# Up projection of a gated MLP: one 512-column matmul over both halves of the activation, and a convolution that reads SBUF

## The reference

```python
def dwconv2d_grid(x, w):
    B, T, C = x.shape
    rows = T // GRID_W                        # GRID_W = 64
    y = lax.conv_general_dilated(x.reshape(B, rows, GRID_W, C), w[:, :, None, :],
                                 window_strides=(1, 1), padding=((1, 1), (1, 1)),
                                 dimension_numbers=('NHWC', 'HWIO', 'NHWC'),
                                 feature_group_count=C)
    return y.reshape(B, T, C)

def conv_glu_ffn(h, w_up, conv_w, w_down, grid):
    up = h @ w_up                             # (256, 2048) @ (2048, 11264)
    up = dwconv2d_grid(up, conv_w)
    a, b = jnp.split(up, 2, axis=-1)
    return (jax.nn.silu(a) * b) @ w_down      # (256, 5632) @ (5632, 2048)
...
h2 = rmsnorm(x, g_pre2) * (1.0 + sc2) + sh2
x = x + gt2 * rmsnorm(conv_glu_ffn(h2, w_up, conv_ffn, w_down, grid=True), g_post2)
```

## Time and profile before

| | |
|---|---|
| median of the runs | 2902.12 us |
| the profiled execution | 2901.94 us, span 2899.9 us |
| TensorE busy | 2783.1 us, 96% |
| VectorE busy | 1893.0 us, 65% |
| ScalarE busy | 996.5 us, 34% |
| GpSimd busy | 567.7 us, 20% |
| TensorE clock granted, mean | 0.982 of full |
| up stage | from 2111.8 us to 2626.9 us |

### The profile page before, as it was taken

One profiled execution on the slowest core, in us unless ns is written; L12 is line 12 of the kernel. 1 busy time (PEld: TensorE's weight loads), 2 busy tenths in 40 slices (PEclk: granted clock), 3 DMA queues, 4 the chain that ended last, 5 costly groups with the idle time before them and its releaser, 6 DMA issues.

```text
span 2899.9 us, 66324 instructions
## 1 busy us (share of the span) xinstructions
PE 2783.1 (96%) x25890; PEld 2094.7 (72%) x25890; DVE 1893.0 (65%) x3509; ACT 996.5 (34%) x1684; POOL 567.7 (20%) x708
## 2 busy tenths in 40 slices
PE   5899999999999999999988999999899999999997
PEld 1346666656666665666655888887789999998886
DVE  1136776666777666777675656564588999896444
ACT  1133333233333223333221433333344444443332
POOL 0012322223321222331220200000023333330000
PEclk8899999999999999999999999999999999999999
DMA  8721233321223322223234545554535555554554
GB/s 329 325 81 57 89 103 110 104 97 57 88 96 110 110 96 65 83 88 110 81 105 157 191 163 193 181 188 168 187 123 182 186 178 186 177 184 160 185 183 138
DMA packets 75801, 412.84 MB, mean 142 GB/s; under 512 B 9296, under 2 KB 11984, under 8 KB 42608
## 3 DMA queue, kind: packets, MB, share of 16 engines
q1 hardware_dynamic: 74864, 408.10, 40.5%
q0 software_dynamic: 768, 2.10, 0.2%
HBM read 405.38 MB, written 4.19 MB: 141 GB/s over the span
## 4 chain that ended last, share of the span: by engine, by line
PE 90%; DVE 4%; DMA 2%; ACT 2%; issue 1%; SPq 0%; DVEq 0%; ACTq 0%; PEldq 0%
PE PB L714 21%; PE Q L977 12%; PE Q L972 6%; PE PB L972 4%; PE PB L967 4%; PE CH L972 3%; PE PB L968 3%; PE CH L967 3%; PE CH L968 3%; PE Q L850 3%; PE Q L836 3%; DMA ring<-w_mod_dram 2%; PE Q L857 2%; PE CH L891 2%; PE CH L873 2%; PE CH L901 1%
## 5 line engine op out<-in xcount | busy, mean ns | idle before, releaser
L714 PE MATMUL PB<-hT,ring 128*128 128x512 f32 (+1 forms) x1536 | 670.7, 551 | 1.0
L1703 DVE TENSOR_TENSOR w_lo_r<-ring,w_hi_r 128x1536 fp32r<-128x1536 f32 (+3 forms) x178 | 389.9, 2190 | 204.4 <-ACT w_hi_r L1290 204.4
L1290 ACT ACTIVATE w_hi_r<-ring 128x2048 fp32r<-128x2048 f32 (+2 forms) x178 | 325.8, 1830 | 314.2 <-PE PB L972 104.0
L714 PEld LDWEIGHTS PB<-hT,ring 128*128 128x128 f32 x1536 | 256.1, 189 | 114.3 <-issue 69.8
L968 PE MATMUL PB<-hT_r,w_hi_r 128*128 128x256 f32 x832 | 204.7, 286 | 0.0
L1989 POOL TENSOR_TENSOR w_lo_r<-ring,w_hi_r 128x512 fp32r<-128x512 f32 x88 | 118.1, 1342 | 356.9 <-ACT w_hi_r L1290 356.9
L1878 DVE TENSOR_TENSOR w_lo_r<-ring,w_hi_r 128x1408 fp32r<-128x1408 f32 x62 | 100.7, 1626 | 131.9 <-ACT w_hi_r L1409 131.9
L1558 DVE SCALAR_TENSOR_TENSOR arena<-ring,csilp,arena 128x512 f32<-128x512 f32 x240 | 180.5, 752 | 6.1 <-DMA ring<-w_mod_dram 1.5
L967 PE MATMUL PB<-hT_r,w_hi_r 128*128 128x256 f32 x704 | 175.9, 289 | 2.8 <-DVE hT_r L1805 2.8
L977 PE MATMUL Q<-ff_r,w_hi_r 128*128 128x512 f32 x704 | 174.4, 395 | 3.5 <-ACT w_hi_r L1409 3.5
L967 PE MATMUL CH<-hT_r,w_hi_r 128*128 128x256 f32 x704 | 170.9, 283 | 0.0
(11 more groups left out here) (268 smaller groups left out, 5335.8 us busy)
## 6 DMA issues: line engine op xcount, KB each, us to landing
ring<-w_up_dram SPq DMA_DIRECT2D x88, 1024.0 KB, 4.8
ring<-w_mod_dram SPq DMA_DIRECT2D x128, 512.0 KB, 3.6
ring<-w_rkv_dram SPq DMA_DIRECT2D x48, 1024.0 KB, 6.0
ring<-w_down_dram SPq DMA_DIRECT2D x64, 704.0 KB, 4.0
ring<-w_mod_dram SPq DMA_DIRECT2D x32, 1024.0 KB, 9.3
ring<-w_ga_dram SPq DMA_DIRECT2D x16, 1024.0 KB, 4.8
ring<-w_gb_dram SPq DMA_DIRECT2D x16, 1024.0 KB, 4.9
ring<-w_pa_dram SPq DMA_DIRECT2D x16, 1024.0 KB, 4.9
```

The costliest lines, as they stand in the source:

```text
L714: last = mm(PB[slot % 2][:, 0:cols], tile(n, kt), hT[:, kt, 0:cols], start=(kt == 0), stop=(kt == KT - 1))
L1290: f(w_hi_r[:, r % 2, 0:n], ring[:, r, 0:n], ACT.Copy).then_inc(hi_rdy, 1)
L1703: tt(w_lo_r[:, r, 0:n], ring[:, r, 0:n], as_f32(w_hi_r[:, r % 2, 0:n]), ALU.subtract).then_inc(lo_rdy, 1)
```

## The change

Each tile of the up stage takes its high part by 16 matmuls of 512 columns over both parts of the activation (columns 0 to 255 of the bank get high·low, columns 256 to 511 high·high), and the low part is added in columns 256 to 511. ScalarE copies columns 0 to 255 into a new SBUF buffer `us[r]` (memory of `woven_sb`), and VectorE adds columns 256 to 511 to it (`add_halves`). The centre tap (ScalarE) and the eight other taps (VectorE) then read `us[r]` in SBUF. TensorE gets the bank back after that addition (`up_sum`). Before a pair's centre taps ScalarE waits for both additions.

```diff
+        us = [woven_sb[:, r].rearrange("p c t -> p (c t)")[:, 0:T] for r in range(4)]
...
-                    pe.wait_ge(up_cv, i * 2 + 1 + r // 2)
+                    pe.wait_ge(up_sum, i * 4 + r + 1)
                     for kt in range(KT):
                         if first and r == 0:
                             pe.wait_ge(h_rdy, KT + kt + 1)
-                        with_high(four[r][:, 0:T], r, kt, h2_hi_r[:, kt], h2_lo_r[:, kt], kt == 0)
+                        mm(four[r][:, :], w_hi_r[:, r % 2, kt * P:(kt + 1) * P], hT_r[:, kt], start=(kt == 0), stop=False)
...
-                        last = with_low(four[r][:, 0:T], r, kt, h2_hi_r[:, kt], kt == KT - 1)
+                        last = with_low(four[r][:, T:TT], r, kt, h2_hi_r[:, kt], kt == KT - 1)
...
                     if r % 2 == 0:
+                        act.wait_ge(up_cv, i * 2 + r // 2 + 1)
+                    f(us[r], four[r][:, 0:T], ACT.Copy).then_inc(up_half, 1)
+                    if r % 2:
                         act.wait_ge(ff_rdy, i * 2 + r // 2 + 1)
-                    f(cv[r], four[r][:, 0:T], ACT.Identity, scale=convw_a[:, r, 4:5]).then_inc(up_mid, 1)
+                        for q in (r - 1, r):
+                            act.wait_ge(up_sum, i * 4 + q + 5)
+                            f(cv[q], us[q], ACT.Identity, scale=convw_a[:, q, 4:5]).then_inc(up_mid, 1)
...
-                        last = stt(grid(cv[r])[:, orow, ocol], grid(four[r][:, 0:T])[:, irow, icol],
+                        last = stt(grid(cv[r])[:, orow, ocol], grid(us[r])[:, irow, icol],
                                    convw_v[:, r, w:w + 1], grid(cv[r])[:, orow, ocol], ALU.mult, ALU.add)
...
+            def add_halves(i, r):
+
+                dve.wait_ge(up_half, i * 4 + r + 1)
+                tt(us[r], us[r], four[r][:, T:TT], ALU.add).then_inc(up_sum, 1)
...
                 if carry is not None:
                     dve.wait_ge(dve_step, V.base)
                     taps(i - 1, 1, 1, carry)
+                add_halves(i, 0)
+                add_halves(i, 1)
                 lows("up", i, 0, FT // 2, "down")
...
                 taps(i, 0, 1, prev)
+                add_halves(i, 2)
+                add_halves(i, 3)
                 lows("up", i, 2, FT // 2, "down")
```

More of the change, by code:

```diff
@@ L354, in layer_kernel @@
         xr_ld = sem("x_reloaded")
+        up_half = sem("up_low_activation_half_copied")
+        up_sum = sem("up_halves_added")
         up_mid = sem("up_centre_tap_done")
@@ L1068, in _ @@
             pe.sem_inc(up_cv, 2)
+            pe.sem_inc(up_sum, 4)
             pe.sem_inc(ff_rdy, 2)
@@ L1813, in taps @@
             def taps(i, j, half, prev):
-                if half == 0:
-                    dve.wait_ge(up_mid, i * 4 + 2 * j + 2)
                 for n in range(4 * half, 4 * half + 4):
@@ L1823, in taps @@
                         ocol, icol = slice(max(0, -b), GRID - max(0, b)), slice(max(0, b), GRID - max(0, -b))
-                        if n:
+                        if n == 0:
+                            dve.wait_ge(up_mid, i * 4 + r + 1)
+                        else:
                             V.need(prev[q])
                         w = 3 * (a + 1) + b + 1
-                        last = stt(grid(cv[r])[:, orow, ocol], grid(four[r][:, 0:T])[:, irow, icol],
+                        last = stt(grid(cv[r])[:, orow, ocol], grid(us[r])[:, irow, icol],
                                    convw_v[:, r, w:w + 1], grid(cv[r])[:, orow, ocol], ALU.mult, ALU.add)
```

## The result

The changed kernel takes 2952.8 us (median of 4 runs, 2951.37 to 2955.72), beside 2902.2 us of the kernel before in the same comparison: ratio 1.0171, 95% interval 1.0157 to 1.0185, or 50.6 us more. Forecast were 2963 us and a range of 2915 to 2992. The profiled execution took 2955.72 us, with a span of 2952.8.

The account below looks back on a forecast made before the run. TensorE bounds the up stage before; then VectorE, 19.9 us of work plus 6.0 for GpSimd, 25.9 us a group against 23.04. Over 22 groups 63 us, less 3, plus 1: +61, so 2963 us, range 2915 to 2992.

Parts of the forecast that it names:

- TensorE's part: Up stage: wider matmuls give back 0.19 us a tile, 17 us over 22 groups, if TensorE stays the bound.
- VectorE's own work: Up stage: 18.5 us of present work plus 1.4 of new additions make 19.9 us a group.
- The price of the additions: Up stage: four new additions a group at 0.34 us each, 1.36 us a group, all on VectorE's line.
- Taps out of SBUF exclude GpSimd: Up stage: VectorE taps with both tensors in SBUF and GpSimd instructions reading SBUF shut each other out for the whole instruction.
- For nearly every GpSimd instruction: Up stage: 18.4 of VectorE's 19.9 us need both tensors from SBUF, so nearly every GpSimd instruction costs its full price.
- GpSimd's term: Up stage: four weight parts at 1.08 us and two activation splits at 0.25 + 0.58 cost VectorE 6.0 us a group.
- The upper bound of the term: GpSimd's cost to VectorE in the up stage is at most 6.6 us a group, cast 0.40, weight parts 1.14 each.
- The ends: Up stage: 3 us taken off for the first and last groups, 1 us added at the end for the last taps.
- Signs that were forecast: Up stage: VectorE never idle, TensorE about 86% busy, GpSimd's weight parts 1.4 to 1.7 us, some taps 0.8 to 1.5.
- Half the price: Rival: weight parts cost 0.54 us each, GpSimd 3.8 us a group in the up stage; +15 us, 2917 us; chance 0.12.
- TensorE stays the bound: Rival: GpSimd costs at most 2.14 us a group, VectorE needs 22.0 against 22.28; 17 us faster, 2885 us; chance 0.08.
- slower than the sum: Rival: SBUF taps cost 0.03 us more each, GpSimd 6.6 us a group; +94 us, 2996 us; chance 0.06.

Follow-up runs that it names:

- e3: Kernel before with the 512-column matmuls alone, high weight by low activation left out, no additions: 2886.35 us, ratio 0.9944 to the kernel before.
- e1: Changed kernel with the sum of the halves written back into PSUM, where all taps read it: 2887.62 us, ratio 0.9954 to the kernel before.
- e5: Kernel before plus one VectorE addition for each tile, into a buffer nobody reads: 2906.29 us, ratio 1.0004.
- e8: Changed kernel without GpSimd's weight parts, four matmuls reading the first four blocks instead: 2889.58 us, ratio 0.9949 to the kernel before.
- e2: Kernel before, with ScalarE also copying each tile into SBUF, where the eight taps read it; no additions: 2926.66 us, ratio 1.0086.
- e6: Changed kernel with VectorE making all 2048 columns of each low part and GpSimd none: 2910.78 us, ratio 1.0024 to the kernel before.
- e7: Changed kernel with 1024 instead of 512 columns of each low part on GpSimd: 3002.09 us, ratio 1.0338 to the kernel before.

## Why the prediction was right, and where its sizes were off

- *TensorE's part* (0.19 us a tile, 17 us): right. e3 measured 16 us, and the groups of e1 are 22.27 us apart where 22.28 were forecast.
- *VectorE's own work* (19.9 us a group): right. 25.3 less the 5.4 of stretched taps leave 19.9, and e1, where nothing is stretched, has VectorE busy for 19.9 us a group.
- *The price of the additions*: they cost nothing alone (e5), since VectorE's line stays under TensorE's 23.04 us.
- *Taps out of SBUF exclude GpSimd*: right; e1 takes it away by the place, e8 by the other side, and e2 makes it alone. *For nearly every GpSimd instruction*: right. In the changed kernel each of them stretches a tap.
- *GpSimd's term* (6.0 us a group) was too large: it is 5.4. A weight part costs a tap 1.45 - 0.41 = 1.04 us (forecast 1.08), the subtraction 0.89 - 0.41 = 0.48 (0.58), the cast 0.61 - 0.47 = 0.14 (0.25, chosen without a row). 4 x 1.04 + 2 x 0.48 + 2 x 0.14 = 5.4. Over 22 groups the difference is 13 us. The upper bound of the term was added up a little too high: 4 x 1.14 and 2 x 0.98 are 6.5 us and not 6.6.
- *The ends* were too small in both directions, and partly made up for each other. The first and last groups gave back 4.3 us (45.2 instead of 49.5) where 3 were taken off, and behind the up stage came 5.8 us where 1 was put on. The longer wait at the start of the down stage and the lower clock behind it are in no term of the sum. That the forecast is only 10 us from the result, with 13 us too much in the groups, owes something to that.
- *Signs that were forecast*: VectorE without idle time, TensorE waiting for low parts, the other taps at 0.41 us, the clock at 1.00 within the up stage, all seen. A tap beside a cast takes 0.61 us, under the forecast 0.8. TensorE busy for 86% was not a good sign. The window has 92%, in part because matmul records overlap (0.39 us each at a pace of 0.23), so that the last one before a wait reaches into it. By tiles it is 4 x 5.57 of 25.3 us, 88%. GpSimd's weight parts at 1.4 to 1.7 us hold for three of four, and the fourth mostly takes 4.99 us.
- *Half the price* failed because the weight parts meet taps and not splits; *TensorE stays the bound* because the taps do exclude GpSimd; *slower than the sum* because an undisturbed tap out of SBUF costs the same (0.41 us) and the term is under its upper bound.

The Trainium skill's rule ("SBUF — State Buffer", section "SBUF: two separate sides") that a VectorE instruction with two SBUF inputs and a GpSimd instruction that reads SBUF shut each other out is what these runs show. A tap of 192 columns beside a weight part takes 1.45 us with both tensors in SBUF (changed kernel), and 0.41 with one of them in PSUM (e1).

## What to carry to other kernels

When an operand moves from PSUM to SBUF, look at GpSimd's instructions in the same stretch: on a nearly full VectorE each one can take a good part of its length from VectorE (here 1.04 of 1.29 us), though instruction counts and undisturbed durations say that the move is free. If the sum of two PSUM halves is read many times by VectorE, try writing it back into PSUM. Here that turned 50 us lost into 15 us won. Work given to GpSimd to relieve VectorE did the opposite once all taps read SBUF: taking it back saved 42 us (e6), and giving more cost 49 (e7). What it is worth while the taps read PSUM was not tried.

## What the runs showed that was not expected

Which of the two engines goes next is not settled by whose record began first. At 2401.77 a GpSimd part began while a tap had just begun (2401.76), and four more taps, a split of 1.75 us and a product went ahead of it. It was done at 2406.76, after 4.99 us instead of 1.29. This happens to one of the four parts in 18 of the 22 groups. The other three get in at the next boundary between two taps that follow each other just as closely. It isn't bound to the weight part: in e8, 14 of 42 casts took 2.67 us and the others 0.70. What decides was not tried.

The median of GpSimd's part (line L2007, ns min/median/max) hides it, and the maximum shows it:

```profile
L2007 POOL TENSOR_TENSOR w_lo_r<-ring,w_hi_r x88: 1288/1421/4987, 2087.1 to 2667.2; 128x512 fp32r<-128x512 f32 x88
```

TensorE lost little by it: it waited for GpSimd's part 17 times, 2.8 us in all.
